# A two-layer trunk on one core: attention's units in one run over the token tiles, and the first experts' weights requested slot by slot

## What is computed

```python
def odd_attend(q_c, k_c, v_c, q_d, k_d, v_d, lam_p, lam_init, subln_g, w_out):
    o_c = blocked_attention(q_c[:, :, None], k_c[:, :, None], v_c, (NOPE_C + ROPE_C) ** -0.5)[:, :, 0]
    o_d = blocked_attention(q_d, k_d, v_d, DH_D ** -0.5)
    ...
    o_d = rms_norm(o_d[:, :, 0] - lam * o_d[:, :, 1], subln_g) * (1.0 - lam_init)
    return jnp.concatenate([from_heads(o_c), from_heads(o_d)], axis=-1) @ w_out
...
        x = x + g1 * mix.astype(x.dtype)
        h = rms_norm(x, norm_g[li, 1]) * (1.0 + sc2) + sh2
        x = x + g2 * moe(h, ...)
```

## Time and profile before

| | us |
|---|---|
| median of 3 runs | 1674.84 (1674.28 to 1678.19) |
| the profiled execution | 1665.2 |
| its span | 1663.5 |
| busy: TensorE products / weight loads | 1367.2 / 924.6 |
| busy: VectorE / ScalarE / GpSimd | 527.0 / 340.4 / 164.3 |
| attention of layer 1, from its first scores | 1137 to 1270 |
| output projection of layer 1 | 1278 to 1328 |

### The profile page before, as it was taken

One profiled execution on the slowest core, in us unless ns is written; L12 is line 12 of the kernel. 1 busy time (PEld: TensorE's weight loads), 2 busy tenths in 40 slices (PEclk: granted clock), 3 DMA queues, 4 the chain that ended last, 5 costly groups with the idle time before them and its releaser, 6 DMA issues.

```text
span 1663.5 us, 38961 instructions
## 1 busy us (share of the span) xinstructions
PE 1367.2 (82%) x16856; PEld 924.6 (56%) x16856; DVE 527.0 (32%) x1193; ACT 340.4 (20%) x704; POOL 164.3 (10%) x238
## 2 busy tenths in 40 slices
PE   4979859988988569899877849977788989987782
PEld 2447824457878334789744424444455479964441
DVE  1324431235444343501111124545455351111013
ACT  2222201132222102300000012433353220000001
POOL 1012310013333000010000012010000010000001
PEclk9999959999999769899998978986789989999897
DMA  9756172420000550779999966114230087999994
GB/s 382 268 190 177 39 254 102 151 102 3 3 3 3 192 234 0 326 283 400 388 403 390 418 231 233 51 65 152 105 134 16 13 373 291 390 398 393 399 411 181
DMA packets 42267, 355.56 MB, mean 214 GB/s; under 512 B 5691, under 2 KB 10635, under 8 KB 23824
## 3 DMA queue, kind: packets, MB, share of 16 engines
q1 hardware_dynamic: 21456, 302.11, 46.0%
q0 software_dynamic: 8864, 29.38, 5.3%
q10 hardware_dynamic: 11808, 22.03, 4.2%
HBM read 322.48 MB, written 31.01 MB: 212 GB/s over the span
## 4 chain that ended last, share of the span: by engine, by line
PE 65%; DMA 17%; DVE 8%; issue 6%; ACT 3%; SPq 1%; ACTq 0%; POOL 0%; POOLq 0%; DVEq 0%
PE PB L622 60%; DMA arena<-in_w_moe 7%; PE PB L625 6%; DMA ring<-in_w_moe 5%; DVE arena L1799 5%; DMA ring<-in_w_mod 3%; ACT arena L1383 1%; DMA arena<-expert_out,rows_i 1%; DMA arena<-in_rw_g 1%; DVE arena L1806 1%; DVE small L1812 1%; DVE x L1799 0%; SPq L398 0%; ACT hT L1383 0%; DVE arena L1809 0%
## 5 line engine op out<-in xcount | busy, mean ns | idle before, releaser
L622 PE MATMUL PB<-arena 64*64 64x64 f32 (+6 forms) x9570 | 504.0, 299 | 82.4 <-DMA arena<-in_w_moe 34.3
L622 PEld LDWEIGHTS PB<-arena 64*64 64x64 f32 (+3 forms) x9570 | 393.8, 133 | 181.3 <-issue 54.3
L622 PE MATMUL PB<-ring,hT 128*128 128x512 f32 (+1 forms) x720 | 315.8, 595 | 6.2 <-DVE hT L1802 3.6
L622 PE MATMUL PB<-ring,arena 128*32 128x256 f32 (+2 forms) x3648 | 221.1, 391 | 37.7 <-DMA ring<-in_w_moe 31.3
L622 PEld LDWEIGHTS PB<-ring,hT 128*128 128x128 f32 x720 | 138.6, 195 | 168.3 <-issue 160.8
L622 PEld LDWEIGHTS PB<-ring,arena 128*32 128x32 f32 x3648 | 156.6, 113 | 94.0 <-DMA ring<-in_w_moe 38.2
L1383 ACT ACTIVATE arena<-PB 128x256 f32<-128x256 f32 (+5 forms) x222 | 104.3, 470 | 406.2 <-PE PB L622 340.4
L625 PE MATMUL PB<-cst,arena 128*128 128x128 f32 (+2 forms) x758 | 122.7, 301 | 75.1 <-DVE arena L1803 25.4
L625 PEld LDWEIGHTS PB<-cst,arena 128*128 128x128 f32 (+2 forms) x758 | 93.3, 158 | 117.9 <-issue 33.3
L2185 DVE TENSOR_TENSOR arena<-arena,PB 128x256 f32<-128x256 f32 (+1 forms) x32 | 15.1, 471 | 353.0 <-ACT arena L1629 353.0
L622 PE MATMUL PB<-ring,scT 128*32 128x512 f32 x384 | 66.6, 835 | 39.7 <-DMA ring<-in_w_mod 39.6
(11 more groups left out here) (142 smaller groups left out, 938.5 us busy)
## 6 DMA issues: line engine op xcount, KB each, us to landing
ring<-in_w_moe SPq DMA_DIRECT2D x48, 2048.0 KB, 15.8
arena<-in_w_moe SPq DMA_DIRECT2D x48, 2048.0 KB, 17.2
ring<-in_w_mod SPq DMA_DIRECT2D x24, 2048.0 KB, 8.2
ring<-in_w_mix SPq DMA_DIRECT2D x22, 2048.0 KB, 8.1
dispatched<-gate ACTq DMA_DIRECT2D x1, 8320.0 KB, 39.0
arena<-dispatched POOLq DMA_DIRECT2D x20, 256.0 KB, 9.0
expert_out<-gate ACTq DMA_DIRECT2D x1, 3456.0 KB, 15.5
expert_out<-arena ACTq DMA_DIRECT2D x12, 288.0 KB, 10.2
```

The source lines that it names most:

```text
L622: return nc.tensor.matmul(out, lhsT, rhs, start=start, stop=stop, **k)
```

## The change

Attention. `values` and `out` of a tile's last unit move to the next tile's first unit, like all others. The closing of tile `t` is spread over the next tile's units: the squares in its unit 0 (`u` = 16, 32), root and second half of the norm in unit 1 (17, 33), transposes and copies in unit 3 (19, 35). Tile 2 is closed after the loop; its transposes stand in `out_projection` behind tile 0's second half, and its copies in `residual` behind the diagonals. `mix` becomes two buffers, at a place that only attention uses then. The factor `1 - LAM_INIT` is applied to the four roots and not to 512 values.

Weights. SyncE requests them in another order. Layer 0: the first expert's down weights when slot 2 and `units1` are done, the second expert's three at the end of `out_g1`, the first's gate and up when slots 0 and 1 are free. Layer 1: the second expert's at the end of `attend` (a new mark on three engines), then the first's three when the ring is free.

```diff
@@ arena @@
-        mix = u0[:, 0:1024]
+        mix = [sq2[:, 0, :], sq2[:, 1, :]]
@@ SyncE @@
-            def weights(L, l, i, c, b, e):
-                for m in range(3):
+            def weights(L, l, i, c, b, e, parts=range(3)):
+                for m in parts:
...
-                for m in range(SLOTS):
-                    if owner[m] is not None:
-                        sp.wait_ge(*when(*owner[m]))
-                    owner[m] = None
+                def slots_free(*slots):
+                    for m in slots:
+                        if owner[m] is not None:
+                            sp.wait_ge(*when(*owner[m]))
+                        owner[m] = None
                 if l == 0:
+                    slots_free(2)
                     meet(sp, "sp", "units1", ("pe", "act", "dve", "pool"))
-                weights(L, l, None, 0, 0, 0)
-                meet(sp, "sp", f"mixer{l}")
-                if l:
+                    weights(L, l, None, 0, 0, 0, (2,))
+                    meet(sp, "sp", "out_g1")
+                else:
+                    meet(sp, "sp", "attend")
                     sp.wait_ge(sem("st_cache"), 14 * 16)
                 weights(L, l, None, 1, 1, 1)
+                slots_free(0, 1, 2)
+                weights(L, l, None, 0, 0, 0, (0, 1) if l == 0 else (0, 1, 2))
@@ TensorE, out_projection @@
+                        if l and j == 0 and n == 1:
+                            odd_mixed_T(2)
@@ TensorE, attend @@
-                    if u % 16:
+                    if u:
                         values(u - 1)
...
-                    if u % 16 == 15:
-                        values(u)
-                        t = u // 16
-                        mixed_T(("omix1", t), lambda k: mix[:, 128 * k:128 * k + 128], t, 1)
+                    if u in (19, 35):
+                        odd_mixed_T(u // 16 - 1)
+                values(47)
@@ ScalarE @@
-                        if m:
+                        if u:
                             weights_T(u - 1)
-                        if m == 15:
-                            weights_T(u)
-                        if m == 15:
-                            root("dd", u // 16)
+                        if u in (17, 33):
+                            root("dd", u // 16 - 1)
+                    weights_T(47)
+                    root("dd", 2)
@@ VectorE, residual @@
                 diagonals(l, 0)
+                if l:
+                    mixed(1, 2)
@@ VectorE, attend @@
+                def squares(t):
+                    od, tmp = h8(mix[t % 2][:, 512:1024], 4), h8(hd[:, 0:512], 4)
+                    tt(tmp, od, od, ALU.mult)
+                    red(small[:, 0:4], tmp)
+                    ts(small[:, 0:4], small[:, 0:4], 1.0 / 128, EPS, ALU.mult, ALU.add, "var", "dd", t)
+
+                def subnorm(t):
+                    od, r = h8(mix[t % 2][:, 512:1024], 4), small[:, 0:4]
+                    dve.wait_ge(*when("root", "dd", t))
+                    step(V.reciprocal(r, r))
+                    ts(r, r, 1.0 - LAM_INIT, None, ALU.mult, None)
+                    tt(od, od, bc(r, 2, 128), ALU.mult)
+                    tt(od, od, bc(R(rowsO, "diff_subln_g"), 1, 4), ALU.mult, "omix1", t)
...
-                    if u % 16 == 15:
-                        out(u)
-                        t = u // 16
-                        od = h8(mix[:, 512:1024], 4)
-                        head_norm(od, h8(hd[:, 0:512], 4), 4, 128, R(rowsO, "diff_subln_g"), "dd", t)
-                        ts(od, od, 1.0 - LAM_INIT, None, ALU.mult, None, "omix1", t)
-                        mixed(1, t)
+                    if u in (16, 32):
+                        squares(u // 16 - 1)
+                    if u in (17, 33):
+                        subnorm(u // 16 - 1)
+                    if u in (19, 35):
+                        mixed(1, u // 16 - 1)
+                out(47)
+                squares(2)
+                subnorm(2)
```

More of the change, by code:

```diff
@@ L1239, in pairs_T, with odd_mixed_T @@
                 ins.then_inc(*tick("pe", out + "_p", t))
+            def odd_mixed_T(t):
+                mixed_T(("omix1", t), lambda k: mix[t % 2][:, 128 * k:128 * k + 128], t, 1)
             def attend():
@@ L1365, in _ @@
                     attend()
+                    end("pe", "attend")
                 out_projection(l)
@@ L1755, in _ @@
                            bias=small[:, 64 + u % 4:65 + u % 4], scale=scale, accum_out=small[:, 240 + u % 4:241 + u % 4])
-                        if m:
+                        if u:
                             weights_T(u - 1)
-                        if m == 15:
-                            weights_T(u)
-                        if m == 15:
-                            root("dd", u // 16)
+                        if u in (17, 33):
+                            root("dd", u // 16 - 1)
+                    weights_T(47)
+                    root("dd", 2)
+                    end("act", "attend")
                 gate_rows(l, 0)
@@ L2363, in out @@
                     if m < 8:
[L2364 removed]
+                        ts(mix[t % 2][:, 64 * m:64 * m + 64], PB[:, 4 + u % 2, 0:64], rec, None, ALU.mult, None, "ov", u)
                         return
[L2366 removed]
+                    o = mix[t % 2][:, 512 + 128 * ((m - 8) // 2):640 + 128 * ((m - 8) // 2)]
                     if m % 2 == 0:
@@ L2467, in _ @@
                     attend()
+                    end("dve", "attend")
                 residual(l)
```

4 lines of the change are left out of this document (1 added, 3 removed).

## The result

The changed kernel takes 1660.11 us at the median (1659.61 to 1666.12), the kernel before 1674.84; the ratio is 0.9925, with a 95% interval of 0.9902 to 0.9947: 12.6 us less by the ratio, 8.9 to 16.4. On another chip, beside the kernel before, it took 1661.57 us, a ratio of 0.9914 (0.9891 to 0.9937). The forecast was 1652.9, with a range of 1645 to 1665, so the time lies inside. Of the gain of 21.9 us that was forecast, two thirds arrived by the medians (14.7) and rather less by the ratio.

A forecast was written before the change was run, and what follows sets the result against it. TensorE's three tile-end waits on VectorE in layer 1's attention (19.9 us), with slow clock behind them, were taken as the bound. Boundary gains 7.2 + 6.5 + 8.2 = 21.9 us, weights nothing: 1674.84 - 21.9 = 1652.9 us, range 1645 to 1665.

The forecast's parts named there:

- rival 1: Attention's tile boundaries: old waits turn into new ones from added VectorE and ScalarE work; gain about 12, time 1663; chance 0.14.
- signs of being right: Trace marks: three 7 us waits gone, new wait about 2 us, projection starting promptly, tile 2's clock above 0.9, ScalarE-bound first product.
- first sign of being wrong: Layer 1's attention shortened by less than 10 us.
- Tile 2 to the projection: End of layer 1's attention: output projection starts right behind the last values, gate products follow VectorE's diagonals; gain 8.2 us.
- Tile 1 to tile 2: Second boundary in attention: unit 34 turns 10.65 us after unit 31 instead of 19.0; net gain 7.2 us.
- I charge 1.2 for both: Unit 35: mixed rows' transposes at full clock, 1.04 us, plus next scores' wait for VectorE's copies; 1.2 us off the gain.
- Tile 0 to tile 1: First boundary in attention, at slow clock: unit 18 turns 13.7 us after unit 15 instead of 21.45; net gain 6.5 us.
- rival 2: Attention: TensorE reaches 2.4 GHz soon after 1180, shortening modulation rows and scores; gain 27, time 1648; chance 0.10.
- Rival 4: Tiles 1 and 2: clock stays down behind ScalarE's table load; all of tile 1 slow loses 10 us, time 1685; chance 0.04.
- Rival 5: ScalarE in attention: four table switches each cost another 1.28 us to empty the engine; 5.1 us lost, time 1658; chance 0.03.
- The weights: Experts' start: earlier requests gain nothing, as ScalarE releases the first product; bounds 4.9 us gain per layer, 5 us loss.
- The shift of 9.6 us: Whole kernel: median 1674.84 lies 9.6 above the profiled execution's 1665.2; assumed to carry over unchanged.

The follow-up runs named there:

- after's second: Second trace of the changed kernel, nothing altered, on chip B: 1661.57 us, 0.9914 of the kernel before.
- before's third trace: The kernel before, unaltered, traced a third time, on chip C: 1675.62 us for its single run.
- filler run: Changed kernel plus 18 unread 128x128 products on TensorE ahead of the turns of units 18 and 34: 1650.17 us, 0.9849 of the kernel before.
- second trace of before: The kernel before, unaltered, run again on chip A: 1665.25 us, 0.9961 of its 25 other runs.
- the kernel with the hold: Changed kernel with SyncE's reload of the third expert's weights held until the scatter of dispatched rows has landed: 1656.27 us, 0.9855 of the kernel before.

## Why the prediction was right or wrong, point by point

- **Range and sign** held. The median was to fall by 21.9 us and fell by 14.7; the traces give 11.0 in attention and about nothing elsewhere (after's second against before's third trace, both gapless: 0.2 more and 1.4 less in the experts). These two spans differ by 16.7 us, of which 4.0 lie ahead of request 0, where nothing but SyncE's requests is changed. That the time fell inside the range was in part luck: two of the three terms of the sum, 13.7 us together, gave 2.8, and the range reached that far for the sake of rival 1, whose reason did not occur. Of the signs of being right one failed: the granted clock from 1226 to 1270 was 0.81, not above 0.9. Attention, shortened by 11.0 us, was 1 us away from the first sign of being wrong.
- **Tile 2 to the projection: 8.2 forecast, 8.2 measured.** The projection started at 1271.77 against an end of the last values at 1271.92; the gate products ended 3.9 us after the first block (3.3 forecast).
- **Tile 1 to tile 2: 7.2 forecast, 0.0 measured.** The step up to unit 34's turn was right: 10.2 us after unit 31's (1226.87 to 1237.06), against 10.65. What failed is the next one: "I charge 1.2 for both", for all that lies between that turn and the end of the tile. It took TensorE to be at full clock there; the granted clock was 0.54 from 1236 to 1254. I had read in the trace that the clock is low for 4 to 6 us behind each wait, and had charged the old waits with it but not the new one of 2.3 us, which I took for a cost of 2.3 us. The filler run put this term at 6.2.
- **Tile 0 to tile 1: 6.5 forecast, 2.8 measured.** The same step. Here two misreadings lie beside it. "TensorE is at 1.2 GHz before and after the wait" is wrong for the time before it: the granted clock of before is 1.00 from 1174.8 on, and the turn of 0.27 us that heads is at full speed (one like it takes 0.42 at 1174.37). So in after the modulation rows took 1.92 us instead of 3.64 (rival 2), and unit 18 turned 9.8 us after unit 15 instead of 13.7. The fall behind the wait took that back and more. And "4 to 6 us behind each wait" was too short for this boundary: behind its old wait before works at 0.50 for 11.2 us. The filler run, with the clock kept, gives 9.1.
- **Rival 1** came true in its size (a gain of 12 by waits that turn into new ones), not by its reason: TensorE waits for VectorE's added work nowhere in after. Its arithmetic doesn't come out either: 1.66 + 2.2 + 1.4 against 1.2 and 2.0 is 2.1 us for a boundary, not 3. Its last half sentence, "a few more by repeated slow clock", was the case. **Rival 4** had the mechanism, a tile that runs at 1.2 GHz behind ScalarE's table load, as a whole tile or nothing; it was 17 us of a tile, twice. The two should have been one rival with a price by the us of slow clock.
- **Rival 5**, a table switch that costs more than its load: no. The copy ends at 1187.45, the load runs from 1187.46 for 1.28 us, the exponential begins at 1188.76. The Trainium skill, page "ScalarE: Activation LUTs", section "What ACT_TABLE_LOAD costs", has 1283 ns and a drain of about 1380 ns; this trace agrees with the first and shows nothing of the second, as the earlier trace rows had it.
- **The weights: nothing, and nothing was measured.** The first product waits for ScalarE in every trace. The sign that I had named as wrong, a first product that no longer leaves TensorE idle, did appear in after, but it appears with old requests as well. What I had not seen is that the reload of the third expert's weights and the scatter share the DMA engines. The Trainium skill, page "DMA: Bandwidth & Descriptors", section "Queues, rings and completion order", says that each engine takes turns between the queues it has work for, packet by packet. The traces agree in so far as the two slow each other, a landing of 4.3 us alone and of 15.1 to 17.3 with the reload beside it; the turns by packet they don't show.
- **The shift of 9.6 us** was carried over as it was. It is not a constant: the second trace of before, 6.9 us longer than the first, has 6.6 of that ahead of request 0, the third, 10.4 us longer, in part there and in part in the experts. No run shows what it was made of in the first set of runs.

## What to carry to other kernels

Price a wait of TensorE with the clock behind it: here 2.3 us of waiting cost some 6 us in the traces of after and 2.5 to 5 in another, and useless products in its place were worth 12.5 us for two waits. A step that moves off the critical path into a full pipeline, such as a root that needs two table loads, must be asked what idle time it leaves there and how long. And when two traces of different kernels differ in a stretch that the change doesn't touch, take a second trace of the old one first: the collision that I had put down to the early requests was in the kernel before too, and one wait on SyncE removed it.

## What the runs showed of the hardware

The same product with the same traffic beside it ran in two ways. In the first 5 us from the first scatter on, the DMA share is 0.63 in before (thinned) as in after and in the kernel with the hold (gapless); in the next 5 it is 0.96 in before and in the kernel with the hold:

```profile
704.00:709.00 5.00, 4.72 (x66) 3.14 (x57) 1.81 (x7) 0.00 (x0) 3.95 (x4) 1.00 0.63 246
709.00:714.00 5.00, 3.48 (x34) 1.87 (x32) 0.00 (x0) 0.00 (x0) 1.92 (x2) 1.00 0.96 376
```

```profile
707.40:712.40 5.00, 5.00 (x98) 5.00 (x89) 1.80 (x7) 0.00 (x0) 3.95 (x4) 1.00 0.63 247
712.40:717.40 5.00, 5.00 (x49) 4.80 (x44) 0.55 (x1) 0.49 (x1) 1.92 (x2) 1.00 0.96 377
```

Before leaves TensorE 1.5 us idle in the second stretch, for "issue" and no wait; the kernel with the hold, 0.0. So the amount of traffic is not what decides. The thinned product was seen on chip A in four traces, and the gapless one on B and C in eight; the two traces whose chip isn't known have one of each, and that is all that the runs tell of the cause. The other pair, some 28.5 instead of 33.4 us for tile 0 with nothing changed in it, goes with the granted clock in the middle of that tile; the short one appeared in three traces of fourteen, on chips A and B.
